# Two weight chunks of the second tile move behind the last expert, and five projections of the first tile with them

## The reference

```python
def peer_ffn(h, ...):                      # block one, second half
    ...                                    # idx: 8 heads x 16 experts for each token, g: their shares
    u_sel = peer_u[idx]
    act = jax.nn.gelu(jnp.einsum('chkd,cd->chk', u_sel, hc)) * g
    v_sel = peer_v[idx]
    return jnp.einsum('chk,chkd->cd', act, v_sel)

def even_layer(x, ...):
    h = rmsnorm(x, ln)
    aq, ak, av, az, bq, bk, bv, bz = split_cols(h @ w_in, EVEN_SPLITS)      # 8 x 512 columns
    ...
    return x + mixed @ w_out

def odd_layer(x, ...):
    h = rmsnorm(x, ln)
    cq, ck, cv, cz, dq, dkc, dvc, dks, dvs, dkw, dvw, dz, dg = split_cols(h @ w_in, ODD_SPLITS)
    oc = moba_attention(cq, ck, cv)                       # each with its norms
    od = nsa_attention(dq, compress(dkc), compress(dvc), dks, dvs, dkw, dvw, sigmoid(dg))
    mixed = jnp.concatenate([oc * jax.nn.silu(cz), od * jax.nn.silu(dz)], axis=-1)
    return x + mixed @ w_out
```

## Time and profile before

| | |
|---|---|
| median of 3 runs | 1218.93 us (1217.1 to 1220.67) |
| the profiled execution | 1214.53 us, of which the trace's span is 1212.9 us |
| mean granted clock of TensorE | 0.955 of full speed |
| busy in the span | TensorE 86%, VectorE 63%, ScalarE 43%, GpSimd 25% |
| HBM | 395 MB, 326 GB/s in the mean |

### The profile page before, as it was taken

The page is one execution under the profiler, slowest core; times in us unless marked ns, Lnnn a source line. Parts: engine busy times, 40 slices in busy tenths (PEclk is TensorE's granted clock), DMA queues, the critical chain, the costliest instruction groups (busy, mean ns, idle before and its releaser), DMA issues.

```text
span 1212.9 us, 11894 instructions
## 1 busy us (share of the span) xinstructions
PE 1041.7 (86%) x3616; PEld 530.2 (44%) x3616; DVE 765.1 (63%) x2013; ACT 525.0 (43%) x1367; POOL 308.3 (25%) x297
## 2 busy tenths in 40 slices
PE   4988887898888799886898978799798798899998
PEld 4755553433334344332344443344343344454564
DVE  5864645689998675568766777786666443242354
ACT  5331139834434534344645563455574213211332
POOL 0000112443445353335332323334234000000000
PEclk9998999999999989999898988999899899999999
DMA  8042798799999999999999999999999574437630
GB/s 315 12 163 79 299 403 328 268 414 414 360 403 374 426 421 424 423 423 420 406 428 426 424 422 367 411 426 419 425 422 421 204 277 156 200 148 277 235 150 18
DMA packets 51727, 395.21 MB, mean 326 GB/s; under 512 B 5536, under 2 KB 10400, under 8 KB 11472
## 3 DMA queue, kind: packets, MB, share of 16 engines
q0 software_dynamic: 37536, 270.91, 54.8%
q1 hardware_dynamic: 13552, 122.83, 25.2%
q10 hardware_dynamic: 576, 0.72, 0.2%
HBM read 393.38 MB, written 1.05 MB: 325 GB/s over the span
## 4 chain that ended last, share of the span: by engine, by line
PE 36%; DMA 19%; DVE 14%; ACT 6%; issue 3%; POOL 0%; DVEq 0%; ACTq 0%; POOLq 0%
DMA expert_rows<-in_peer_uv,peer_idx 18%; PE bank L1783 15%; PE bank L1445 11%; DVE expert_rows L1390 6%; PE bank L2015 2%; PE bank L2056 2%; PE bank L1654 1%; PE bank L1690 1%; PE bank L2031 1%; DVE r L973 1%; ACT L1513 1%; PE bank L1157 1%; ACT L1424 1%; ACT peer_diag L1431 1%; ACT peer_dots L1425 1%
## 5 line engine op out<-in xcount | busy, mean ns | idle before, releaser
L1445 PE MATMUL bank<-expert_rows,peer_diag 128*128 128x512 f32 x896 | 450.9, 637 | 96.4 <-ACT peer_diag L1431 96.2
L1458 POOL DMA_INDIRECT expert_rows<-in_peer_uv,peer_idx x256 | 296.1, 1157 | 531.9 <-PE bank L1445 436.6
L1390 DVE CUSTOM_DVE_ANT_0 expert_rows<-expert_rows,HN 128x1024 f32<-128x1024 f32 x256 | 309.8, 1221 | 123.9 <-DMA expert_rows<-in_peer_uv,peer_idx 122.7
L1445 PEld LDWEIGHTS bank<-expert_rows,peer_diag 128*128 128x128 f32 x896 | 169.9, 200 | 320.2 <-issue 165.3
L1783 PE MATMUL bank<-w_ring,b_xt 128*128 128x512 f32 (+1 forms) x576 | 275.7, 603 | 9.2 <-ACT b_sq L1814 4.4
L1424 ACT ACTIVATE peer_dots<-peer_dots 128x1 f32<-128x1 f32 x256 | 51.7, 202 | 332.1 <-DVE peer_dots L1390 331.3
L1783 PEld LDWEIGHTS bank<-w_ring,b_xt 128*128 128x128 f32 x576 | 105.5, 196 | 114.7 <-issue 107.0
L1431 ACT ACTIVATE peer_diag<-ident,peer_dots 128x128 f32<-128x128 f32 x224 | 89.9, 401 | 7.3
L1425 ACT ACTIVATE peer_dots<-peer_dots,peer_ex 128x1 f32<-128x1 f32 x256 | 75.4, 295 | 8.3
L1513 ACT ACT_TABLE_LOAD x53 | 68.0, 1283 | 18.6 <-DMA x_res<-in_x 5.6
L1424 ACT ACT_TABLE_LOAD x48 | 61.6, 1283 | 14.2 <-DVE peer_dots L1390 13.4
(11 more groups left out here) (389 smaller groups left out, 1141.0 us busy)
## 6 DMA issues: line engine op xcount, KB each, us to landing
w_ring<-in_w_in_e SPq DMA_DIRECT2D x16, 2048.0 KB, 11.5
w_ring<-in_w_in_o SPq DMA_DIRECT2D x14, 2048.0 KB, 11.4
w_ring<-in_w_query SPq DMA_DIRECT2D x8, 2048.0 KB, 10.1
w_ring<-in_w_out SPq DMA_DIRECT2D x4, 2048.0 KB, 8.6
w_ring<-in_w_out_e SPq DMA_DIRECT2D x4, 2048.0 KB, 11.0
w_ring<-in_w_out_o SPq DMA_DIRECT2D x4, 2048.0 KB, 7.3
w_ring<-in_w_in SPq DMA_DIRECT2D x2, 2048.0 KB, 15.6
expert_rows<-in_peer_uv,peer_idx POOLq DMA_INDIRECT x256, 12.3
```

The costliest lines, as they stand in the source:

```text
L1390: t.dve.tensor_tensor_reduce(u, u, t.HN[:, it // PH, :], 1.0, 0.0, ALU.mult, ALU.add, self.dots[:, it, k:k + 1]).then_inc(*self.dotted.add())
L1445: ins = t.pe.matmul(t.PS[2 * T + c][:, :], self.diag[:, d % self.RD, :], self.slot(n)[:, D + c * 512:D + (c + 1) * 512], start=k == 0, sto ...
L1458: t.pool.indirect_dma_start(self.slot(n), None, t.dram["peer_uv"], bass.IndirectOffsetOnAxis(ap=self.idx[:, it, k:k + 1], axis=0)).then_in ...
```

## The change

A constant `LATE = 3` is passed to `project` for tile 0's odd layer. That generator makes projections 1 to 3 as before, then sets `done["held"]` and stops until `"far"`. The loop over experts no longer asks for tile 1's two chunks. Behind the loop, SyncE waits for the landing of the last gather but one and issues them then. Projections 4 to 8 of tile 0, with what hangs on them, are written out beside tile 1's even layer. They all use bank `L.pa`, and the late gates and the sigmoid use the form with Exp and Ln that tile 1 uses, in place of Tanh.

```diff
@@ -36,6 +36,8 @@
 
 CHUNK = 512
 RING = 3
+
+LATE = 3
 SBUF_FROM, SBUF_TO = 16512, 229344
 
 SG = 32
@@ -1748,7 +1750,8 @@
     return led(L, pe(), dve(), act())
 
 
-def project(L, matrix, jobs):
+def project(L, matrix, jobs, late=None):
+
 
     t, T = L.t, L.T
     sigged = L.sem("p_sigged")
@@ -1761,22 +1764,29 @@
         plan.append((c, n, kind, to, count[what] if what else 0, count["taken"]))
         if what:
             count[what] += 1
+    soft = [T == 0 and (late is None or j < late) for j in range(len(plan))]
     emptied = [shut.at(j + 1) if kind == "add" else taken.at(got) for j, (_, _, kind, _, _, got) in enumerate(plan)]
     banks = [L.pa] + [L.spare] * (L.spare is not None)
     nb = len(banks)
     before = dict(L.free)
+    where = [j % nb if late is None or j < late else 0 for j in range(len(plan))]
+    prior = [max([i for i in range(j) if where[i] == where[j]], default=None) for j in range(len(plan))]
     for j, e in enumerate(emptied):
-        L.free[j % nb] = e
+        L.free[where[j]] = e
 
     def pe():
         for j, (c, n, kind, _, _, _) in enumerate(plan):
+            if j == late:
+                L.done["held"] = True
+                while "far" not in L.done:
+                    yield
             while not t.w.ready(T, matrix, c):
                 yield
             i = t.w.take(T, matrix, c, n)
             if j == 0:
                 t.pe.wait_ge(*L.done["xt"])
             t.w.wait(t.pe, i)
-            pa, free = banks[j % nb], emptied[j - nb] if j >= nb else before.get(j % nb)
+            pa, free = banks[where[j]], emptied[prior[j]] if prior[j] is not None else before.get(where[j])
             if free is not None:
                 t.pe.wait_ge(*free)
             for k in range(KT):
@@ -1797,7 +1807,7 @@
                 continue
             for _ in range(L.lead):
                 yield
-            ps = banks[j % nb]
+            ps = banks[where[j]]
             if j == 0:
                 t.act.wait_ge(*L.done["rstd"])
             t.act.wait_ge(*summed.at(j + 1))
@@ -1812,7 +1822,7 @@
                 if m:
                     t.act.wait_ge(*reduced.at(m))
                 t.act.activation(L.sq[:, 0:w], ps[:, 0:w], ACT.Square, scale=rstd).then_inc(*taken.add())
-            elif kind == "gate" and T == 0:
+            elif kind == "gate" and soft[j]:
                 t.act.wait_ge(*(shut.at(m) if m else reduced.at(count["heads"])))
                 gelus(t)
                 t.act.activation(L.sq[:, :], ps[:, :], ACT.Tanh, scale=half)
@@ -1825,8 +1835,8 @@
             elif kind == "sig":
                 t.act.activation(to, ps[:, 0:256], ACT.Copy, scale=rstd)
                 sig = L.sig[:, :, :].rearrange("p h c -> p (h c)")
-                (logs if T else gelus)(t)
-                how = (ACT.Exp, minus) if T else (ACT.Tanh, half)
+                (gelus if soft[j] else logs)(t)
+                how = (ACT.Tanh, half) if soft[j] else (ACT.Exp, minus)
                 t.act.activation(sig, ps[:, 256:280], how[0], scale=how[1]).then_inc(*taken.add())
             else:
                 t.act.activation(to, ps[:, 0:n], ACT.Copy, scale=rstd).then_inc(*taken.add())
@@ -1841,7 +1851,7 @@
                 logs(t)
                 t.ach.step(t.act.activation(L.hs[:, m, sl], L.hs[:, m, sl], ACT.Ln, bias=t.col("eps"), scale=1.0 / DH))
                 t.act.activation(L.rs[:, m, sl], L.hs[:, m, sl], ACT.Exp, scale=-0.5).then_inc(*rooted.add())
-            elif kind == "gate" and T:
+            elif kind == "gate" and not soft[j]:
                 yield
                 t.act.wait_ge(*opened.at(m + 1))
                 logs(t)
@@ -1857,7 +1867,7 @@
             if kind == "add":
                 x = t.X[:, T, c:c + n]
                 t.dve.wait_ge(*summed.at(j + 1))
-                t.dve.tensor_tensor(x, banks[j % nb][:, 0:n], x, ALU.add).then_inc(*shut.add())
+                t.dve.tensor_tensor(x, banks[where[j]][:, 0:n], x, ALU.add).then_inc(*shut.add())
                 L.done["x"] = L.done["x", c // 512] = shut.at(j + 1)
                 continue
             t.dve.wait_ge(*taken.at(got))
@@ -1893,7 +1903,7 @@
                 L.done["gate", to] = shut.at(m + 1)
             else:
                 sig = L.sig[:, :, :]
-                if T == 0:
+                if soft[j]:
                     t.dve.tensor_scalar(sig, sig, 1.0, 0.5, ALU.add, ALU.mult).then_inc(*sigged.add())
                 else:
                     t.dch.step(t.dve.tensor_scalar(sig, sig, 1.0, None, ALU.add))
@@ -2534,7 +2544,7 @@
         t.pool.wait_ge(*L.done["x"])
         join(L, ("ok0", "os0", "oj"), [(K[0], K[1], n) for K, n in ((od.K, "ok"), (od.KS, "oks"), (od.KW, "oks"))])
     yield from turn_x(L, "ln_o")
-    yield from woven(L, one_by_one(lambda: and_beside(L, asked(L, project(L, m, jobs)), turn_half(L, t.PS)),
+    yield from woven(L, one_by_one(lambda: and_beside(L, asked(L, project(L, m, jobs, (LATE, None)[T])), turn_half(L, t.PS)),
                                    lambda: first_half(L, "w_out_o", t.PS)),
                      stream(L, items, outs, Compress(L, od, od.w2)), rate)
     yield from odd_gates(L, acc)
@@ -2715,13 +2725,14 @@
         t.w.pump(t.sp)
         if n > 100 and wanted and t.w.open() and t.w.next == len(t.w.loads):
             t.w.ahead(0, *wanted.pop(0))
-        if n > 140 and "asked" in lanes[0].done and len(then) and t.w.open():
-            t.w.ahead(1, *then.pop(0))
+    t.sp.wait_ge(*peer.arrived(peer.NI * TOPK - 2))
+    while then and t.w.open():
+        t.w.ahead(1, *then.pop(0))
     for engine in (t.pe, t.dve, t.act, t.sp, t.pool):
         engine.wait_ge(*peer.total.at(2 * QT))
     for a, m in ((t.bias[1][:, :, :], "alibi"), (t.count[1][:, :], "count"), (od.cbias[:, :, :, :], "cbias"), (od.pe_in[:, :, :], "phi_pe"), (od.w2[:, :, :], "phi_w2")):
         t.sp.dma_start(a, dram[m]).then_inc(t.bias_in, 16)
-    while "asked" not in lanes[0].done:
+    while "held" not in lanes[0].done:
         next(ahead)
     t.pe.wait_ge(*lanes[0].free[1])
     lanes[0].spare, lanes[0].lead, lanes[0].done["far"] = None, 0, True
```

## The result

The changed kernel takes 1275.99 us (median of 4 runs, 1274.24 to 1283.22); the kernel before, run beside it, 1218.01 us (1214.43 to 1220.67). The ratio is 1.0471, with a 95% interval of 1.0434 to 1.0508: 4.7% slower. The prediction was 1263 us, range 1230 to 1286.

A forecast was written before the change was run, and what follows sets the result against it. It took the expert stage as bound by DMA bytes and what follows by TensorE. Expert stage -29.5, TensorE work +43.0, net chunk waits +22.6 and clock +8.3 gave +44 us on the median 1218.93: 1263 us, range 1230 to 1286.

The forecast's parts named there:

- Expert stage, -29.5: Stage of tile 1's experts: without the seven moved weight chunks the gathers have DMA alone, 29.5 us gained.
- The two counts agree within 3 us: Expert stage: 29.5 us left over beside 51 dot products at 2.48 us, against 32 us for 13.7 MB of chunks.
- Rival D: Expert stage doesn't shorten because something other than bytes paced it: +74 us, 1293 us; chance 0.05.
- TensorE work, +43.0: Behind the experts: tile 0's moved projections (32.4 us) and attention (10.6) land where TensorE is the limit.
- The first wait, 12.9: Tile 1's input transposes: TensorE waits 12.9 us for tile 0's fourth chunk, queued behind tile 1's two chunks and the tables.
- Chunks 7 and 8, 3.2: Tile 0's late projections: waits of 3.6 and 2.8 us after cover by tile 1's matmuls, half of that taken.
- What these waits cover, -10.3: Behind the experts: new chunk waits cover old ones, 2.5 us at the transition, 4.4 for squares, 3.4 for w_out_o.
- The clock, +8.3: TensorE behind the experts: clock drops of 3.3 us behind four chunk waits, less 4.9 already paid, +8.3 us.
- Banks, +3 set against idle time: Tile 1's odd layer starts without the second PSUM bank: two waits of 1.45 us, set against 8 us idle.
- A: Behind the experts: only the first wait stays, later chunks land in time; +16 us, 1235 us; chance 0.17.
- B: Behind the experts: moved work fills idle TensorE time and no chunk is late; -5 us, 1214 us; chance 0.08.
- C: Behind the experts: each wait drops the clock, no old idle time is covered, missing bank costs 3; +64, 1283 us; chance 0.12.

The follow-up runs named there:

- e8: Kernel before, with the seven chunks the change moves bringing one of eight row groups (12 MB less), all work in its old place; 1211.75 us, ratio 0.9932.
- e6: e4, with tile 0's late projections making one of their eight matmuls each; 1230.69 us, ratio 1.0084.
- e3: Changed kernel, with the chunk of tile 0's fourth projection issued ahead of tile 1's two; 1262.53 us, ratio 1.0369.
- e12: Kernel before, with the edits of e8 and e9 both at once; 1211.87 us, ratio 0.993.
- e9: Kernel before, with all bytes loaded but one matmul of eight in tile 0's last five odd projections; 1222.67 us, ratio 1.0004.
- e4: Changed kernel, with w_in_e and w_in_o chunks from tile 0's fourth on bringing one of eight row groups, all matmuls made; 1252.38 us, ratio 1.0267.
- e7: Changed kernel, with 14 useless matmuls put ahead of the first wait so that TensorE works through it; 1273.97 us, ratio 1.0448.
- e10: Changed kernel with LATE = 6, so only the two gate projections of tile 0 are late; 1253.77 us, ratio 1.0279.

## Why the prediction was right, by its steps

**Expert stage, -29.5: -27.9.** The size was right and the reason half right. The pace of 2.48 us for an expert beside gathers alone was read from a stretch where the attention was gone as well as the chunks; so the estimate held for this change, which takes both away. It would have failed for a change of the bytes alone: for the 12 MB of e8 it says 28 us, and e8 gave 10.9. That the size came out is in part luck. "The two counts agree within 3 us" was the wrong comfort. The share of 0.98 and the 13.7 MB were true, and yet the bytes were not the only limit. Rival D was put at 0.05 as if either bytes or something else paced the stage; in fact both did.

**TensorE work, +43.0.** The 168 records that the two stretches gained are exactly those I had counted: 80 of projections and 88 of the attention. Their price of 43.0 us is that of before, at its clock; no run measures it apart. e6 took 28.4 us of it away and the time fell by 22.3.

**The first wait, 12.9: 14.0, and the queue behind SyncE as its cause** (e3: gone when the chunk goes first). **Chunk 5, 7.3: 7.2. Chunk 6 and tile 1's chunk 3, 9.5: 5.5 + 3.5 = 9.1. Chunks 7 and 8, 3.2: 2.5 + 2.0.** In sum 34.7 for 32.9. Counting from the DMA that leaves only when a ring place is freed, with the landing time from the trace of before, gave each wait within 1.5 us; halving the last two, as I did, took them too low.

**What these waits cover, -10.3: this was the step that was mis-sized.** Of the three old waits two went: the 3.4 us for `w_out_o` and the 2.5 at the transition. The 2.60 us at 925.87 are another wait, for the last addition of the experts; it was 1.47 in before and is 2.5 and 2.9 in e8 and e12, so it isn't the change's. ScalarE's squares were not covered: 5.9 us in five times, where I counted 4.4 as gone. And new waits came, of 1.4, 1.2, 1.0 and 3.3 us between 1106 and 1117. All but the first belong to the last heads of tile 0's second attention, on its compressed keys (`o_ckk`, `o_kcn`). In before this work stood near 1000 us without such waits; now it ends beside tile 1's last even heads, with little other matmul work between them:

```profile
1106.77 1.13 PE L2066 MATMUL bank<-e_V,b_pT 128*128 128x128 f32 x8 [1.40 <-DVE b_o L2132]
...
1117.03 1.84 PE L2025 MATMUL bank<-o_kcn,b_Q 64*128 64x7 f32 x8 [3.33 <-DVE b_mn L2091]
```

TensorE's waits for anything but chunks sum to 23.0 us from 924 on. In before they were 19.2 from 952 on, and I had taken 6.9 off them. TensorE's idle time grew by 35.5 us and not by 22.6. The span grew by 61.2 us, 17 more than the 44 of the sum: 13 from the idle time, 2 from the clock, 1.6 from the experts. The median missed by 13, because I had lifted the forecast by the 4.4 us by which the profiled execution of before was faster than its median.

**The clock, +8.3.** TensorE's busy time grew by 53.6 - 43.0 = 10.6 us more than the work that moved. 3 to 6 of these may be the spread between executions: with the same 976 or 977 records TensorE is busy 234.8 us in before and 237.7 to 240.9 in e8, e9 and e12. e4, which shortens the chunk waits, gives 8.9 back. So the size stands, loosely. Around the second and third wait the granted clock is low as forecast, with columns as in the earlier trace rows, which these two answer:

```profile
963.00:971.00 8.00, 7.22 (x13) 3.22 (x14) 0.00 (x0) 0.00 (x0) 0.00 (x0) 0.71 0.00 0
984.00:992.00 8.00, 3.23 (x5) 1.40 (x6) 0.00 (x0) 0.00 (x0) 0.00 (x0) 0.55 1.04 441
```

Full speed is the upper of the two levels (2.4 GHz), 0.5 the lower. The Trainium skill (TensorE: Matmul & The Clock Gate, "Loop structure matters more than you think") says that matmuls go to the lower level behind a long wait for a DMA; that the wait be long is a condition that the prediction left out. The traces agree that the clock fell at each of the first three waits (0.57 in the first, 0.71 and 0.55 around the next two). e7, which fills the longest of them, gives back 1.7 us in the 16.5 us behind it; the whole time, 2.8 us with overlapping intervals, doesn't narrow this. So for this wait the price may be nearer 2 us than the 3.3 that I took from one case.

**Banks, +3 set against idle time.** TensorE waits for squares 5.9 us in five times, 1.5 us more than before's three. That is half of the price I had named, and the idle time did not take it up: another part of the mis-sized cover.

**Rivals.** A (the ring keeps up) falls: the waits are there one by one. B (idle time filled) falls with it. C and the forecast differ in what is covered, and the measured 1276 lies nearer to C (1283). C is half right: 5.9 of the 10.3 us were covered, the missing bank cost 1.5 and not 3, and the clock cost at most 2 more than forecast, not 7. D falls for this change: the stage did shorten by 28.

## What to carry to other kernels

A stage at 0.98 of DMA bandwidth can have a second limit 10 us beneath the first; what a relief is worth is known only from a stretch where everything is relieved that the change relieves, and a change of bytes alone must not be priced by it. When work and its weights move behind a barrier, price each load by when its place in the buffer comes free and by its queue, wait by wait: that was accurate here to 1.5 us. Don't count old waits as covered by new ones unless they stand at the same place in the engine's queue: the one that did was covered here, and the squares were not.

None of the forms tried with late work beats the kernel before (the best, e10, is 2.8% slower, e3 3.7%). Moving tile 1's two chunks alone measures 0.2% faster, with an interval that reaches 1.0001, so no gain is shown.

## What had not been expected of the hardware

Each change of ScalarE's function set costs a table load of 1.28 us, and 22 of them stood between 796 and 921 us in before. The Trainium skill (ScalarE: Activation LUTs, "What ACT_TABLE_LOAD costs") gives the same 1283 ns and adds 1.38 us of drain, 2.66 in all for a switch. ScalarE's timeline of e12 agrees with the first and shows no second:

```profile
879.34 0.40 ACT L1433 ACTIVATE peer_diag<-ident,peer_dots 128x128 f32<-128x128 f32 x1
879.75 1.28 ACT L1515 ACT_TABLE_LOAD   x1
881.05 0.40 ACT L2144 ACTIVATE b_s<-b_s,b_mn 128x128 f32<-128x128 f32 x1
```

The load begins as the activation before it ends, and the next activation begins as it ends: 1.31 us from one to the other.

A chunk of 256 KB, in e4, still kept TensorE waiting 9.3 us, because 5.5 MB of other loads were queued ahead of it. And 12 MB of 63 MB taken away from a stage that ran at 0.98 of its DMA share shortened it by 10.9 us, where the bytes at 422 GB/s would be 28.
